# Expert weights of a mixture layer: two chunks of an expert by one transfer of 2 MB instead of two of 1 MB

## What is computed

```python
hg = jnp.einsum('sd,edh->seh', xs, w_gate)      # w_gate: 32 x 1024 x 256
hu = jnp.einsum('sd,edh->seh', xs, w_up)        # w_up:   32 x 1024 x 256
h = jax.nn.silu(hg) * hu * gate[..., None].astype(xs.dtype)
return jnp.einsum('seh,ehd->sd', h, w_down)     # w_down: 32 x 256 x 1024
```

## Time and profile before

| | us |
|---|---|
| median of 3 runs | 2885.62 |
| lowest and highest | 2882.09, 2887.09 |
| the profiled execution, its own time | 2877.1 |
| its span, first to last instruction | 2875.3 |
| mean granted TensorE clock | 0.962 of full speed |
| TensorE busy with products | 2652.2 (92%) |
| GpSimd, VectorE, ScalarE busy | 886.6, 1084.4, 786.1 |
| bytes moved by DMA | 344.15 MB, 120 GB/s on average |

### The profile page before, as it was taken

How to read it: one execution, slowest core, us unless ns; L and a number is a source line. 1 busy time by engine, 2 the same in 40 slices (tenths; PEclk the granted TensorE clock), 3 DMA queues, 4 the chain that set the end, 5 groups by cost and what they waited for, 6 DMA issues and landing times. The chain is left out here.

```text
span 2875.3 us, 31045 instructions
## 1 busy us (share of the span) xinstructions
PE 2652.2 (92%) x12444; PEld 1935.2 (67%) x12444; DVE 1084.4 (38%) x1832; ACT 786.1 (27%) x1123; POOL 886.6 (31%) x273
## 2 busy tenths in 40 slices
PE   7989788999878898599999999999998999999998
PEld 6854436877633333466688888888685788888887
DVE  1156545466331111556644422112366444411111
ACT  1022321143211111432622332222425422322221
POOL 4710000024013222232134444444231344444443
PEclk9989889989879999799999999999999999999999
DMA  4423111043348877323022222222322222222223
GB/s 159 147 85 118 41 48 41 1 155 123 163 154 349 322 303 288 131 100 101 30 103 96 95 94 97 103 89 102 120 92 72 74 89 102 95 96 102 89 103 117
DMA packets 84870, 344.15 MB, mean 120 GB/s; under 512 B 34446, under 2 KB 34830, under 8 KB 49144
## 3 DMA queue, kind: packets, MB, share of 16 engines
q1 hardware_dynamic: 63640, 314.39, 29.7%
q10 hardware_dynamic: 7264, 19.35, 2.1%
q0 software_dynamic: 13824, 8.44, 1.0%
HBM read 385.19 MB, written 28.21 MB: 144 GB/s over the span
## 5 line engine op out<-in xcount | busy, mean ns | idle before, releaser
L159 POOL TENSOR_TENSOR w_lo<-w_raw,w_hi 128x2048 fp32r<-128x2048 f32 x149 | 691.8, 4643 | 1613.3 <-ACT w_hi L152 1566.5
L183 PE MATMUL bank<-xh,w_hi 128*128 128x512 f32 x1704 | 671.9, 394 | 32.5 <-DVE xl L348 19.2
L185 PE MATMUL bank<-xh,w_lo 128*128 128x512 f32 x1704 | 666.7, 391 | 0.0
L184 PE MATMUL bank<-xl,w_hi 128*128 128x512 f32 x1704 | 666.4, 391 | 0.0
L183 PEld LDWEIGHTS bank<-xh,w_hi 128*128 128x128 f32 x1704 | 322.1, 189 | 117.0 <-issue 22.6
L152 ACT ACTIVATE w_hi<-w_raw 128x2048 fp32r<-128x2048 f32 x152 | 290.8, 1913 | 368.1 <-PE bank L183 336.2
L184 PEld LDWEIGHTS bank<-xl,w_hi 128*128 128x128 f32 x1704 | 322.2, 189 | 67.9 <-issue 1.2
L185 PEld LDWEIGHTS bank<-xh,w_lo 128*128 128x128 f32 x1704 | 321.8, 189 | 67.7
L183 PE MATMUL bank<-ha,w_hi 128*128 128x512 f32 x480 | 186.7, 389 | 0.0
L184 PE MATMUL bank<-hb,w_hi 128*128 128x512 f32 x480 | 186.7, 389 | 0.0
L185 PE MATMUL bank<-ha,w_lo 128*128 128x512 f32 x480 | 186.7, 389 | 0.0
(11 more groups left out here) (571 smaller groups left out, 3535.2 us busy)
## 6 DMA issues: line engine op xcount, KB each, us to landing
w_raw<-weights SPq DMA_DIRECT2D x192, 1024.0 KB, 4.8
ring<-weights SPq DMA_DIRECT2D x64, 1024.0 KB, 11.9
res<-weights SPq DMA_DIRECT2D x16, 1024.0 KB, 8.2
early_gates<-gate_rows SPq DMA_DIRECT2D x20, 256.0 KB, 2.0
ahead<-early_gates ACTq DMA_DIRECT2D x20, 256.0 KB, 2.7
res<-xT ACTq DMA_DIRECT2D x2, 2048.0 KB, 9.0
distance_bias<-distance_bias_once ACTq DMA_DIRECT2D x8, 512.0 KB
na_bias<-grid_bias SPq DMA_DIRECT2D x16, 240.0 KB, 4.7
```

Of the source, the lines that this page charges most:

```text
L159: engine.tensor_tensor(self.lo[:, s, :], self.raw[:, s, :], self.hi[:, s, :].bitcast(F32), ALU.subtract).then_inc(self.split, 1)
L183: self.released(pe.matmul(out, hi, moving[0], start=start, stop=False))
L184: pe.matmul(out, hi, moving[1], start=False, stop=False)
L185: return pe.matmul(out, lo, moving[0], start=False, stop=stop)
```

## The change

The buffers are renumbered so that chunks 0 and 1 of one side are neighbours (2 x side + part), and part 2's are 4 + side. A base pass's chunks 0 and 1 of a side come by one transfer of 2 MB into both buffers, with 8 KB runs in memory from each chunk. It is issued where part 1 was, so after the release by the second half of gate_up(b - 2). Both halves of gate_up wait on the semaphores of these two transfers. Part 2 stays two transfers of 1 MB. Overflow passes still load part by part, into the renumbered buffers. The last wait before `ws.load` is for the second half of the last even gate_up instead of the first, since the `w_raw` buffers now hold chunk 1 too.

```diff
-        buffer_of = lambda b, part, side: PASS_CHUNKS * (b % 2) + 2 * part + side
+        buffer_of = lambda b, part, side: PASS_CHUNKS * (b % 2) + (2 * side + part if part < 2 else 4 + side)
+        pairs = {0: ws.raw[:, 0:2, :], 2: ring[:, 0:2, :], 6: ring[:, 4:6, :], 8: ring[:, 6:8, :]}
...
-                engine.wait_ge(chunk_in[buffer_of(b, part, side)], 16 * loads)
+                engine.wait_ge(chunk_in[buffer_of(b, 0 if part < 2 else 2, side)], 16 * loads)
...
             def load(b, part):
                 wait_released(sp, b, part)
                 for side in range(2):
-                    e = PASS_ORDER[b][1] + BASE_PASSES * side
-                    n = buffer_of(b, part, side)
-                    sp.dma_start(slots[n], ws.dram[expert0 + MOE_CHUNKS * e + part, :, :]).then_inc(chunk_in[n], 16)
+                    c = expert0 + MOE_CHUNKS * (PASS_ORDER[b][1] + BASE_PASSES * side)
+                    n = buffer_of(b, 0 if part < 2 else 2, side)
+                    if part < 2:
+                        sp.dma_start(pairs[n], ws.dram[c:c + 2, :, :].rearrange("c p n -> p c n")).then_inc(chunk_in[n], 16)
+                    else:
+                        sp.dma_start(slots[n], ws.dram[c + 2, :, :]).then_inc(chunk_in[n], 16)
...
-            for b, part in ((0, 0), (0, 1), (0, 2), (1, 0), (1, 1)):
+            for b, part in ((0, 1), (0, 2), (1, 1)):
                 load(b, part)
...
-                    for part in range(MOE_CHUNKS):
+                    for part in (1, 2):
                         load(b, part)
-            sp.wait_ge(g_used, 2 * last_even + 1)
+            sp.wait_ge(g_used, 2 * last_even + 2)
             ws.load(sp)
```

## The result

| | before | changed |
|---|---|---|
| median, us (6 runs of each) | 2883.86 | 2893.19 |
| lowest to highest | 2876.25 to 2887.09 | 2890.55 to 2895.36 |
| the profiled execution, its span | 2875.3 | 2893.6 |

What follows compares the result with a forecast made beforehand. Bound: the chain from y_ready through 6 MB of weights, gate_up of b7, then b8 and down(7) to y_ready. Terms -2.9 and +9.8 gave +6.9 us on 2885.62, so 2892.5; own range 2889 to 2895, with rivals 2881 to 2905.

Steps and rivals of the forecast that it cites:

- -2.9: Expert stage: sum in us of later products and vanished overflow stops over the seven measured waits, 1150.3 against 1153.24, clock excluded.
- Number and size of transfers: SP's weight loads: four 1 MB issues per base pass become two of 2 MB; nothing won, stream already at 426 GB/s.
- Joint arrival, 3.46 us in each of seven: gate_up of b4, b7, ... b22: starts only when all 4 MB are there, costing 3.46 us in each of seven passes.
- The overflow stop goes: In front of overflow passes b5, b8, ...: stop and low clock behind it vanish, gaining 1.0 us in each of six groups.
- Clock: TensorE in the seven gate_ups behind longer stops: clock falls in six of seven at 1.63 us, +9.8; bounds 0 to 11.6.
- Release: Pairs of b6 and its like, issued after gate_up(4) ends: cover of 3 to 5 us, cost 0 if it holds.
- Overflow transfers: GpSimd's queue: weight queue runs dry about 2 us earlier than new pairs start, so overflow transfers get through at once.
- End of stage: ws.load after gate_up(22): waits some 5 us longer, to 1134, but its chunks are split past 1153; costs nothing.
- A: TensorE's clock stays up or falls seldom: -2.9 to +2 us, 2883 to 2888; chance 0.22.
- D: Weight loads: fewer, larger transfers save start costs, -10 us; 2872 with the clock high, 2882 with it low; chance 0.13.
- B: GpSimd's queue gets half the turns, so scatter and gather land later: +3 (2895) to +20 us (2913); chance 0.07.
- C: First base passes (b6 and its like) get late, 2 us each in seven: +14 us, about 2906; chance 0.08.

Runs made afterwards that it cites:

- both_small: Kernel before, 1 MB transfers kept, with both the first half's wait for all four chunks and the late release: 2889.89 us, ratio 1.0034.
- sides_pair: Kernel before with 2 MB transfers holding one part of both sides, release and waits by part as before: 2885.34 us, ratio 1.0007.
- the change again: The changed kernel, unaltered, timed again on the same chip as three other kernels: 2893.54 us, ratio 1.0034 to the kernel before.
- wait_all: Kernel before, 1 MB transfers and early release kept; only the first half of a base pass's gate_up waits for all four chunks: 2894.78 us, ratio 1.0038.
- after_filled: Changed kernel with four unused products on TensorE in front of gate_up of b4, b7, ... b22: 2878.01 us, ratio 0.9986 to the kernel before.
- late_release: Kernel before; only part 0's loads wait for the second half of gate_up two passes before, ws.load likewise at the end: 2855.23 us, ratio 0.9903.
- over_first: Kernel before; only SP waits, before the loads of b3, b6, b9, ..., until the previous pass's overflow chunks have landed: 2862.20 us, ratio 0.9934.
- sides_late: Kernel before with 2 MB transfers holding one part of both sides, plus the late release for part 0: 2855.41 us, ratio 0.9907.

## Why the prediction came out as it did

The direction and the mechanism were right: the joint arrival costs, the end of the overflow stops gives about as much back, and the low clock behind the longer stops decides. The sum had two terms, -2.9 and +9.8; the first was right and the second too small, so that the stage is 13.1 us longer and not 6.9. The median moved by 9.3 us (interval 6 to 15), which holds both. That it came out within 1 us of the 2892.5 is in part luck: the forecast started from 2885.62, where the median of six runs is 2883.86, and its clock term was 6.2 us too small for the profiled stage.

1. *Number and size of transfers*: right, nothing that shows, by both_small and sides_pair.
2. *Joint arrival, 3.46 us in each of seven*: right. From the end of down before, y_ready, to gate_up's start it is 878.58 - 859.89 = 18.7 us for b4 and 19.8 for b7; over the seven passes 135.9, the sum that was taken over from before, so the last chunk lands as it did (135.3 to 136.0 in the profiles of the change again, wait_all and both_small). wait_all shows the joint arrival alone. The stops in front of gate_up are 3.9 to 5.0 us long; the prediction said 4.6 to 5.0, though before, in b13, the second half started 5.9 us after the first (996.00 and 1001.89).
3. *The overflow stop goes*: right in the changed kernel, where no stop is left in front of b5 to b20, and right in size: 13.1 less the 16.0 of part 4 leaves the -2.9 that were worked out, and without low clocks (after_filled) the stage is 4.4 us shorter than before. The late release isn't needed for it, as wait_all shows. But the term was costed only inside the change. By itself the end of these stops is worth 26 us, and the change holds an edit that gives them (the late release) and another that takes them and more back. The prediction's "gain 1.0 us in each of six groups" hid that, and so did my expectation of late_release.
4. *Clock*: the mechanism right, the size not. Seven of seven fell, not six, and all but b4's (1.41) cost more than 1.63: gate_up took 8.33 us in b4, 8.79 in b7 and up to 9.67 in b19, 64.4 in the seven, 16.0 over 7 x 6.92. The rows of before that I took the 1.66 from had stops of 2.0 to 3.85 us; here they are 3.9 to 5.0, and the clock stays at 1.2 GHz for longer: 9.67 - 6.92 = 2.75 us lost in b19 means 5.5 us at the low level. A gather's stop shortly ahead doesn't explain it: b13 has none and loses 9.60 - 6.92 = 2.68, b7 has the longest, 2.43, and loses 1.87. Why the loss differs between passes is open. -2.9 + 16.0 = 13.1, the stage's difference. So the step that was off is the bound "all of seven (7 x 1.66 = 11.6)": it took the loss behind one stop as fixed, and 16.0 us lie beyond it.
5. *Release*: right for the change: 3.3 us to spare in b6, no stop there, cost 0. That the later release would be a gain on its own lay in part 6 and was not followed to its price.
6. *Overflow transfers*: right. Those of b5 land at 885.1 to 885.6 in the changed kernel, all four within 0.5 us, once the last weights ahead of them have landed (872.5 + 9.1 = 881.6). over_first shows that this is the place of late_release's gain, for about three quarters of it (20.3 of 27.2 us).
7. *End of stage*: right, nothing; from the end of the last down to the end of the span it is 1722.4 us after and 1722.1 before.

The rivals: A (the clock stays up) is refuted by all seven stops; its price for a kernel without low clocks, -2.9, is near the -4.4 of after_filled. D, that a larger transfer saves something, falls with the seven waits, whose sum stayed at 135.9, and with sides_pair. B, that GpSimd's queue gets half the turns, falls with the landings in sides_pair: one overflow transfer per 2.4 us beside pairs. By the Trainium skill's rule of whole packets ("DMA: Bandwidth & Descriptors", Queues, rings and completion order), as the prediction used it, there would have been half as many. Gather stops are longer with 2 MB in the two pairs of traces with equal waits, by 2.5 us (sides_pair after before) and 3.2 (13.9 in sides_late, 10.7 in late_release), at landings that take as long (9.8 and 9.7, 9.6 and 9.4); what makes them longer is open. C did not happen: 3.3 us were to spare.

## What to carry to other kernels

Before two transfers are joined, ask what each half unlocks and what its release starts: here the size was worth nothing in a stream that already ran at 426 GB/s, while the wait for the whole and the clock behind the longer stop cost 40 us in the stage (late_release to both_small), and a release later by half a pass, which looks like a loss, gained 27. Where transfers are issued by one engine in order, order them by when they are needed; it made the joined transfers harmless. Cost the parts of a change one by one against the kernel before, not only their sum: where a gain and a loss cancel, the gain alone is a kernel that should be tried.

## What the runs showed of the hardware

- The overflow passes load next to nothing in this data: the software queue, through which GpSimd's transfers go, moved 8.44 MB in the kernel before (row q0 of its page). Gathering 2 x 512 rows of 4 KB and scattering as many makes 8.39 of it, an estimate from the shapes. Yet beside a stream of weights each indirect transfer of 128 rows, all out of bounds, took as long as 1 MB of weights, 2.5 us, and no longer beside transfers of 2 MB (sides_pair). In a gap of the stream four of them landed within 0.5 us (late_release). Whether the price goes by rows or by transfers no run here varies.
- TensorE's low clock cost from 1.4 us (b4) to 2.75 us (b19) behind stops of nearly one length, 4.33 and 4.20 us, in the changed kernel. The gather's stop ahead of it doesn't explain the spread: b7 has one of 2.43 us and loses 1.87, b13 has none and loses 2.68. A gather's stop alone was enough for the low level too: 3.00 us in over_first, with a granted clock of 0.50 behind it. What sets it stays open. Four products without use in the stop brought the clock back to 1.00 and 15 us with it.
